# Expert rows gathered as quarters of a row and turned by VectorE, down weights copied by VectorE and ScalarE and asked for one expert later

## The reference, cut to what matters

```python
h_x = modulate(x, norm2_g[i], sf_x, cf_x).reshape(-1, d)      # rms_norm(x, g) * (1 + scale) + shift
scores = sigmoid(t @ router_w); _, idx = top_k(scores + router_bias, 8)   # 64 experts, 8 for each token
y = (silu(t[tok] @ w_gate[e]) * (t[tok] @ w_up[e])) @ w_down[e]           # expert width 256
routed = zeros((n_tok, d)).at[buf_tok].add(y * buf_w[:, None])
```

## Time and profile before

| | |
|---|---|
| median of 3 runs | 2725.13 us (2721.9 to 2731.74) |
| the profiled execution, own time | 2728.36 us |
| its span | 2726.7 us |
| phase `experts`, first ask for weights to last matmul | 1620.4 to 2590.6 |
| PE busy over the span | 91% |
| DMA | 410.21 MB, mean 150 GB/s over the span, some 340 GB/s in the expert phase |

### The profile page before, as it was taken

How to read it: one execution, slowest core, us unless ns; L and a number is a source line. 1 busy time by engine, 2 the same in 40 slices (tenths; PEclk the granted TensorE clock), 3 DMA queues, 4 the chain that set the end, 5 groups by cost and what they waited for, 6 DMA issues and landing times. The chain is left out here.

```text
span 2726.7 us, 72339 instructions
## 1 busy us (share of the span) xinstructions
PE 2492.2 (91%) x27195; PEld 1369.5 (50%) x27196; DVE 1518.7 (56%) x2653; ACT 975.3 (36%) x1707; POOL 842.9 (31%) x654
## 2 busy tenths in 40 slices
PE   5999899889799789899879779899999999999977
PEld 2448457735589645699834343333333333333333
DVE  3106355844477712676544476566666666666538
ACT  3613115512222113233211124455555555555411
POOL 1000000000155100111000005566666666666565
PEclk9999998989999999899979889999999999999989
DMA  6001402120000020000032328899988899684177
GB/s 251 15 0 48 143 16 93 49 64 16 1 4 4 3 75 1 2 5 5 6 137 93 128 103 317 333 352 357 358 337 328 331 343 346 252 312 142 70 282 295
DMA packets 109531, 410.21 MB, mean 150 GB/s; under 512 B 21049, under 2 KB 37131, under 8 KB 84236
## 3 DMA queue, kind: packets, MB, share of 16 engines
q1 hardware_dynamic: 77068, 289.81, 29.0%
q0 software_dynamic: 20736, 75.51, 7.4%
q10 hardware_dynamic: 11520, 41.95, 3.9%
HBM read 347.45 MB, written 59.77 MB: 149 GB/s over the span
## 5 line engine op out<-in xcount | busy, mean ns | idle before, releaser
L3282 PE MATMUL bank<-arena 128*32 x1280 | 568.9, 598 | 10.3 <-SPq L68 7.7
L3284 PE MATMUL bank<-arena 128*32 128x512 f32 x3840 | 570.0, 598 | 0.0
L3243 POOL COPY arena<-arena 128x2048 f32 x240 | 449.2, 1906 | 330.8 <-PE bank L3316 317.6
L3282 PEld LDWEIGHTS bank<-arena 128*32 128x32 f32 x1280 | 134.9, 110 | 359.3 <-issue 350.3
L3313 PE MATMUL bank<-arena 128*32 x640 | 289.3, 595 | 5.5 <-POOL arena L3243 5.5
L3316 PE MATMUL bank<-arena 128*32 128x512 f32 x1920 | 290.3, 595 | 0.0
L3437 DVE COPY arena<-arena 128x2048 f32 x80 | 138.7, 1734 | 203.4 <-PE bank L3284 189.3
L3374 ACT COPY arena<-arena 128x2048 f32 x80 | 152.2, 1902 | 168.5 <-PE bank L3284 141.9
L3233 POOL DMA_INDIRECT arena<-normed_rows,arena x80 | 165.0, 2063 | 118.6 <-DVE arena L3421 106.8
L1262 PE MATMUL bank<-arena 64*64 64x64 f32 x4480 | 165.4, 220 | 13.4 <-DVE arena L1334 5.4
L3313 PEld LDWEIGHTS bank<-arena 128*32 128x32 f32 x640 | 70.4, 110 | 197.8 <-issue 197.1
(11 more groups left out here) (553 smaller groups left out, 4625.7 us busy)
## 6 DMA issues: line engine op xcount, KB each, us to landing
arena<-in_exp_w_gate_dram SPq DMA_DIRECT2D x64, 1024.0 KB
arena<-in_exp_w_up_dram SPq DMA_DIRECT2D x64, 1024.0 KB
arena<-in_exp_w_down_dram SPq DMA_DIRECT2D x64, 1024.0 KB
expert_rows<-arena ACTq DMA_DIRECT2D x80, 512.0 KB
arena<-in_w_mod_dram SPq DMA_DIRECT2D x32, 512.0 KB, 7.7
arena<-in_x_dram SPq DMA_DIRECT2D x16, 512.0 KB
arena<-in_w_mod_dram SPq DMA_DIRECT2D x8, 1024.0 KB, 18.3
arena<-in_w_in_dram SPq DMA_DIRECT2D x12, 384.0 KB
```

Source lines behind the costliest of these rows:

```text
L3243: last = nc.gpsimd.tensor_copy(down_copy(u), down_of(slots[u]))
L3282: nc.tensor.matmul(out(SUB - 1), XTT[:, b.q, c, rows(SUB - 1)], W[:, :, c], start=first, stop=end)
L3284: last = nc.tensor.matmul(out(u), XTT[:, b.q, c, rows(u)], WC[:, u, :, c], start=first, stop=end)
```

## The change

- `mixed_out` puts scale and shift on each row before it is stored: two DVE operations of 128x1024 in place of one, with scale and shift spread over all partitions once at the start (16 matmuls, 8 copies by DVE, 8 by ACT). POOL then reorders each row into four quarters of 256 channels, grouped by `c` (128x1024, once per tile), and SP stores that. The copies out of PSUM lose their scale and shift.
- `IDX` holds four numbers for each row, one per quarter: 16 small DVE operations in place of one.
- In `experts`, POOL gathers 4 x 128 quarters of 1 KB per block, placed so that DVE's 32x32 transpose of 128x1024 gives the columns that `hidden` reads. PE's `turn` and both `flat_half` go.
- POOL's three copies of down weights go; DVE makes one (128x2048, at its step's end) and ACT two.
- SP asks for `down(e-1)` after the gates of `e` have landed, in place of `down(e)` before. At the start it asks for gates 0, down 0 and gates 1, and waits for the first gathered rows before the rest.

```diff
+    by_quarter = lambda row: row.rearrange("p (r i c) -> p r c i", r=SUB, c=KC)
+    packed = lambda row: row.rearrange("p (r c i) -> p r c i", r=SUB, c=KC)
...
+            for t in range(XT):
+                pool.wait_ge(xn, t + 1)
+                if t >= 2:
+                    pool.wait_ge(st[t % 2], 16 * (t // 2))
+                nc.gpsimd.tensor_copy(packed(XP[:, t % 2]), by_quarter(XN[:, t % 2])).then_inc(xp, 1)
...
                     if u >= 2:
                         dve.wait_ge(st[u % 2], 16 * (u // 2))
                         dve.wait_ge(xt, u - 1)
-                    nc.vector.tensor_scalar(XN[:, u % 2], X1[:, u], ri[:, u % 2], None, ALU.mult).then_inc(xn, 1)
+                    if u >= 2:
+                        dve.wait_ge(xp, u - 1)
+                    if u == 0:
+                        dve.wait_ge(mul_in, 1)
+                        dve.wait_ge(add_in, 1)
+                    chain(nc.vector.scalar_tensor_tensor(XN[:, u % 2], X1[:, u], ri[:, u % 2], MULS, ALU.mult, ALU.mult))
+                    nc.vector.tensor_tensor(XN[:, u % 2], XN[:, u % 2], ADDS, ALU.add).then_inc(xn, 1)
                     dve.wait_ge(xt, u + 1)
                     for c in range(KC // 2, KC):
...
+            quarters = IDX[:, 0:NBLK * SUB].rearrange("p (b q) -> p b q", q=SUB)
+            for q in range(SUB):
+                for r in range(SUB):
+                    last = TS(quarters[r * BR:(r + 1) * BR, :, q], ps[0][q * BR:(q + 1) * BR, 0:NBLK], float(SUB),
+                              float(r), ALU.mult, ALU.add)
+            chain(last)
...
     masks = Carve(cr.arena, P)
-    G, XTT, YB = cr.take(2, D), cr.take(2, KC, P), masks.take(2, D)
+    G, XTT, YB = cr.take(2, SUB, D // SUB), cr.take(2, D), masks.take(2, D)
     WC, WDC = cr.take(SUB - 1, 2, KC, ED), cr.take(SUB - 1, 2, D)
     HT, SG, H = masks.take(2, 2, P), masks.take(2, ED), masks.take(2, ED)
-    ID = cr.take(2, 1).bitcast(I32)
+    ID = cr.take(2, SUB).bitcast(I32)
+    row_quarters = xn_dram.rearrange("t (r n) -> (t r) n", r=SUB)
...
+    def columns(b, u, c):
+        at = ((u + 1) % SUB * KC + c) * BR
+        return XTT[:, b.q, at:at + BR]
...
     def slot_of(eng, b, u):
         n = eng.value_load(TAB[0:1, bass.ds(b.n * SUB + u if u else b.n * SUB, 1)], min_val=0, max_val=RING - 1)
         return bass.ds(n, 1)
@@ -3158,53 +3197,58 @@
             def at(i, n):
                 return i * ROUND + n if n else i * ROUND
 
-            def follow(j, i):
-                e, gates, downs = FROM + j, i * DRING, i * RING
+            def gates(i, e):
                 copied, read = released(at(i, e - RING))
                 hold(sp, hi_d, copied)
                 hold(sp, hi_a, copied)
                 hold(sp, up, read)
                 gate_up(bass.ds(at(i, e), 1), e % RING)
-                hold(sp, down_in[(e - 1) % DRING], downs * 16 + (16 * ((e - 1) // DRING) + 16))
+
+            def gates_landed(i, e):
+                hold(sp, loaded[e % RING], i * (DRING * 32) + 32 * (e // RING + 1))
+                sp.sem_inc(arrived, 1)
+
+            def downs(i, f):
+                if f >= DRING:
+                    copied, read = released(at(i, f - DRING))
+                    hold(sp, dcopy_d, copied)
+                    hold(sp, dcopy_a, copied)
+                    hold(sp, dn, read)
+                down(bass.ds(at(i, f), 1), f % DRING)
+
+            def down_landed(i, f):
+                hold(sp, down_in[f % DRING], i * (RING * 16) + 16 * (f // DRING + 1))
                 sp.sem_inc(down_arrived, 1)
-                copied, read = released(at(i, e - DRING))
-                hold(sp, dcopy, copied)
-                hold(sp, dn, read)
-                down(bass.ds(at(i, e), 1), e % DRING)
-                hold(sp, loaded[e % RING], gates * 32 + (32 * (e // RING) + 32))
-                sp.sem_inc(arrived, 1)
-
-            ROUND, FROM = RING * DRING, DRING
+
+            def follow(i, e):
+                gates(i, e)
+                down_landed(i, e - 2)
+                gates_landed(i, e)
+                downs(i, e - 1)
...
+            gate_up(bass.ds(0, 1), 0)
+            down(bass.ds(0, 1), 0)
+            gate_up(bass.ds(1, 1), 1)
+            sp.wait_ge(g_in[0], 16 * SUB)
+            downs(0, 1)
+            gate_up(bass.ds(2, 1), 2)
+            gates_landed(0, 0)
+            down_landed(0, 0)
+            gates_landed(0, 1)
+            gates_landed(0, 2)
+            for e in range(RING, FROM):
+                follow(0, e)
...
             def gather(b):
                 hold(pool, idx, b.n + 1)
-                nc.gpsimd.indirect_dma_start(
-                    out=G[:, b.q], out_offset=None, in_=xn_dram,
-                    in_offset=bass.IndirectOffsetOnAxis(ap=ID[:, b.q], axis=0)).then_inc(g_in[b.q], 16)
-
-            def copy_down(b, n=1):
-                slots = [down_slot_of(pool, b, u) for u in range(SUB - 1)]
-                hold(pool, down_arrived, count_of(pool, b, SUB - 2))
-                if n:
-                    hold(pool, dn, b.n + 1)
-                for u in range(SUB - 1):
-                    last = nc.gpsimd.tensor_copy(down_copy(u), down_of(slots[u]))
-                last.then_inc(dcopy, 1)
+                for q in range(SUB):
+                    nc.gpsimd.indirect_dma_start(
+                        out=G[:, b.q, q], out_offset=None, in_=row_quarters,
+                        in_offset=bass.IndirectOffsetOnAxis(ap=ID[:, b.q, q:q + 1], axis=0)).then_inc(g_in[b.q], 16)
 
             for n in range(4):
                 gather(Turn.at(n))
-            copy_down(Turn.at(0), 0)
-            gather(Turn.at(4))
-            with pool.Fori(0, TRIPS - 2) as t:
+            with pool.Fori(0, NBLK // 2 - 2) as t:
...
             def widen(b):
                 slot = down_slot_of(pe, b, SUB - 1)
                 hold(pe, down_arrived, count_of(pe, b, SUB - 1))
-                hold(pe, dcopy, b.n + 1)
+                hold(pe, dcopy_d, b.n + 1)
+                hold(pe, dcopy_a, b.n + 1)
                 hold(pe, hto, b.n + 1)
                 hold(pe, ya, b.n + 1)
...
+            def copy_downs(b, n=1):
+                slots = [down_slot_of(act, b, u) for u in (1, 2)]
+                hold(act, down_arrived, count_of(act, b, 2))
+                if n:
+                    hold(act, dn, b.n + 1)
+                nc.scalar.copy(down_copy(1), down_of(slots[0]))
+                nc.scalar.copy(down_copy(2), down_of(slots[1])).then_inc(dcopy_a, 1)
 
...
+            def turn(b, n=1):
+                hold(dve, g_in[b.q], b.half * 64 + 64)
+                if n:
+                    hold(dve, up, b.n)
+                nc.vector.transpose(XTT[:, b.q], G[:, b.q].rearrange("p q n -> p (q n)")).then_inc(turned, 1)
+
+            def copy_down(b, n=1):
+                slot = down_slot_of(dve, b, 0)
+                hold(dve, down_arrived, count_of(dve, b, 0))
+                if n:
+                    hold(dve, dn, b.n + 1)
+                nc.vector.tensor_copy(down_copy(0), down_of(slot)).then_inc(dcopy_d, 1)
 
             def index(b):
-                nc.vector.tensor_copy(ID[:, b.q], IDX[:, bass.ds(b.n, 1)]).then_inc(idx, 1)
...
-                    flat_half(b3)
+                    turn(b3)
                 if b5 is not None:
                     index(b5)
+                copy_down(b1)
...
```

More of the change, by code:

```diff
@@ L2736, in turn @@
                 last.then_inc(yt, 1)
+            for n, cols in enumerate((k.mul_col[1][0], k.add_col[1][0])):
+                for c in range(KC):
+                    last = nc.tensor.matmul(ps[4 + 2 * n + c // 4][:, (c % 4) * P:(c % 4 + 1) * P],
+                                            cols[:, c:c + 1].to_broadcast([P, P]), k.ident, start=True, stop=True)
+                last.then_inc(spread, 1)
             turn(0)
@@ L2773, in turned @@
                 nc.scalar.copy(YT[:, t % 2, 0:256], ps[0][:, 0:256]).then_inc(ya, 1)
+            act.wait_ge(spread, 2)
+            for c in range(KC):
+                last = nc.scalar.copy(ADDS[:, c::KC], ps[6 + c // 4][:, (c % 4) * P:(c % 4 + 1) * P])
+            last.then_inc(add_in, 1)
             turned(0)
@@ L2799, in turned @@
                 nc.vector.tensor_copy(YT[:, t % 2, 256:512], ps[1][:, 0:256]).then_inc(yd, 1)
+            dve.wait_ge(spread, 1)
+            for c in range(KC):
+                last = nc.vector.tensor_copy(MULS[:, c::KC], ps[4 + c // 4][:, (c % 4) * P:(c % 4 + 1) * P])
+            last.then_inc(mul_in, 1)
             turned(0)
@@ L3281, in chunk @@
                     first, end = c == 0, c == KC - 1
-                    nc.tensor.matmul(out(SUB - 1), XTT[:, b.q, c, rows(SUB - 1)], W[:, :, c], start=first, stop=end)
+                    nc.tensor.matmul(out(SUB - 1), columns(b, SUB - 1, c), W[:, :, c], start=first, stop=end)
                     for u in range(SUB - 1):
-                        last = nc.tensor.matmul(out(u), XTT[:, b.q, c, rows(u)], WC[:, u, :, c], start=first, stop=end)
```

(1 more changed line is left out.)

138 lines of the change are left out of this document (44 added, 94 removed).

## The result

| | before | change |
|---|---|---|
| median | 2725.9 us (5 runs) | 2841.5 us (2836.7 to 2846.4) |
| ratio | | 1.0409 [1.0388, 1.0430] |
| the same two kernels measured again (e1) | 2725.6 us | 2851.2 us, 1.0459 [1.0426, 1.0493] |
| span of the profile | 2726.7 us | 2842.4 us (e1) |

The change is slower, by 116 us. The profile taken with the first measurement fell into an execution of 12,010 us at a granted clock of 0.19 and says nothing, so the profile after is that of e1, the same kernel.

A forecast was written before the change was run, and what follows sets the result against it. The prediction took PE and the transfers to be balanced in the middle, and PE alone to bind past 2310 us. It summed 94 - 19 + 8 + 3 + 2.5 = +88.5 us on 2728.4, and forecast 2814 us, range 2695 to 2885.

The forecast's parts named there:

- The hole (+94): Small experts, 1684 to 2310 us: late asks leave q1 empty 5.0 us an expert, 14.1 us against 12.27, +94 us.
- The 12.8 us: Cycle per small expert if a transfer's whole fixed cost is about 2.0 us; the sum some 66 us lower.
- PE outside the middle (-19): From 2310 to 2590 us PE binds; 21 turns without transposes save 0.90 us each, -19 us.
- the zero for ACT: Expert turns: ACT's load with two more copies, 10.1 us, fits beside 10.87 and 14.1, so costs nothing.
- the rival without a hole: Middle stretch: transfers bind as now, the cycle stays about 12.0 to 12.3 us an expert, 2720 us; chance 0.15.
- Rival, PE still binds (2662): Middle stretch: the hole is covered, the cycle stays under 11.3 us an expert, 2662 us; chance 0.15.
- Quarters (+8): Expert gathers: 1 KB packets in place of 4 KB rows cost more DMA time, +8 us (0 to 17).
- mixed_out and table (+5.5): Ahead of the experts: added DVE and POOL work in the last tile +3 us, 16 small table operations +2.5 us.
- Start (0): Start of the expert phase: SP's wait for the first gather against 16 transposes no longer awaited, 0, +-5 us.
- POOL (9.9 or 11.0 us a turn): Expert turns: four gathers take POOL 9.9 us, or 11.0 if DVE's copies lengthen them; below the forecast cycle of 14.1.
- Low clock (2941): Middle stretch: every expert's wait drops PE to its low clock, some 2.5 us more a cycle, 2941 us; chance 0.05.

The follow-up runs named there:

- e3: The kernel before with one part alone, down(e-1) asked for only after the gates of e have landed: 2805.0 us, 1.0287.
- e2: The change with SP's asks, the first ones too, in the order of the kernel before: 2773.2 us, 1.0161.
- e5: The change with SP's asks as before, and ACT's table loads for its two copies of down weights put ahead of its store: 2706.6 us, 0.9924.
- e10: The change with SP's asks as before, and the table loads of ACT, PE and SP put ahead of their waits or work: 2682.7 us, 0.9842.
- e7: The change with SP's asks as before and one gather of whole 4 KB rows a block for four of quarters (channels misordered): 2765.0 us, 1.0130.
- e11: The change with its own late order of asks, and the table loads of ACT, PE and SP put ahead: 2737.3 us, 1.0028.

## Why the prediction was right, and where it was not

Forecast 2814 us in 2695 to 2885, slower at 0.70; measured 2841.5. Sign, mechanism and range held. Step by step, against the profile of e1:

- **The hole (+94): right.** 14.07 us an expert for a forecast of 14.1. The hole seen was 4.0 us at 150 GB/s and 1.0 more at 184, for 5.0 at 130. Its parts came out otherwise, and their errors nearly cancel: 3.1 us from last byte to ask for 1.0 + 1.7, and 1.65 from ask to full flow for 2.3. In the rows of before, the reading of the last byte took all of the flow up to 2003.0 for q1's; q1 had nearly run dry at 2002.0, and the rest were gathers (0.37 MB on q0 from 2002 to 2003). In us it gave 82.9 over 52 experts, quarters included, for 94 and 8, because the base was 12.48 and not 12.27 (the larger experts past 2310 us belong to it). e3 has it alone at 79 us, e1 less e2 at 78. The 12.8 us that the prediction drew from a fixed cost of 2.0 us took the shorter hole off and left out that less of q0 and q10 then fits into it: by its own working the estimate is (4.21 - 3.7 x 0.13)/0.391 + 3.7 = 13.2 us, and a sum 44 us lower, not 66. The fixed cost of about 2.0 us is what the Trainium skill (DMA: Bandwidth & Descriptors, Anatomy of one DMA) gives for transfers that GpSimd issues, and these are SP's. The trace does not agree for this chain: with SP's step at the 1.7 us of before, the rest of the hole is an estimated 3.1 - 1.7 + 1.65 = 3.05 us, and the cycle was 14.07.
- **PE outside the middle (-19): wrong, by 34 us, and with it the zero for ACT.** The tail grew by 15.4. The step that failed is "Both fit beside 10.87 and easily beside 14.1, so I cost them at nothing". ACT's 10.1 us was a sum of busy times (8.9 in the turn shown). The turn of ACT is a ring: its work, 1.15 us for DVE's half of the store, 0.6 for PE and 2.1 us of table loads and waits, 12.2 to 12.4 in all (the instructions overlap by some 0.4). The remark that ACT would be late next "with under 2 us to spare" named the engine, but counted no idle time that the engine makes itself. e5 shows it: the 2 us away, the turns are 10.87 to 10.97, as forecast. The middle hid the same fault: e2, without the late asks, would still have been at 12.83 us an expert and not at the 12.0 to 12.3 of the rival without a hole.
- **Rival, PE still binds (2662):** did not happen. e10 comes to 2682.7 with both obstacles gone, at 11.83 us an expert for 11.3.
- **Quarters (+8):** 8 us by e7, not clear of the noise.
- **mixed_out and table (+5.5):** +8.1 (of it the table, 4.91 us for 16 operations against 0.24 [4.7 for a forecast of 2.5, at 0.31 us each and not 0.11 to 0.24], and 3.45 ahead of it, the start of the table's writing against that of before, for 3). Over all profiles of either sort the mean is +11.4, so some 3 us more may be true.
- **Start (0): +9.4.** In e1 SP waited 9.0 us for the first gather before it asked for down 1 and gates 2. e2, which has neither that wait nor late asks, has 64.0, as before. The two were not separated; e3, with late asks from the 7th expert on and no such wait, has 65.9, and e11, with the wait and shorter steps, 66.6.
- **POOL (9.9 or 11.0 us a turn): too high.** A gather took 1277 ns on average, not 2182; the shortest took 942, the longest 2432. That it starts at another moment against DVE's copies, now that POOL's own are gone, was not separated. The Trainium skill (SBUF — State Buffer, SBUF: two separate sides) has a lock that a copy of DVE can hold against GpSimd, and the rows agree in kind: a gather of 1.82 us in e1 (2427.06) ran beside a copy of DVE (2427.53), two of 0.95 beside none. By these numbers it is an estimated 4 x (1.28 - 0.95) = 1.3 us of POOL a turn, and of the time no more than the 8 us of e7.
- **Low clock (2941):** no; the granted clock was 0.95 in the middle, against 0.99 before.

The terms that missed make the difference: 2.6 (ahead) + 9.4 (start) + 34.4 (tail) - 19.1 (middle) = 27.3 us, which is what the forecast of 88.5 lacks to 115.8. So the mechanism of the large term was right, but that the figure came within 28 us was in part luck: the middle came out 19 us under its forecast and the tail 34 us over, and inside the hole two misreadings nearly cancelled.

## What to carry to other kernels

An engine that works in order is late by its ring, not by its busy time: add to its work each wait in it and the time in which its queue reads tables or goes through waits with registers, which the timeline of the engine shows only as idle "on issue". Put such loads ahead of a wait that stands there anyway; here 2 us of them moved by two lines were worth 66 us. And a queue that waits for one transfer before it asks for the next needs something else in flight, enough for the whole step from last byte to next flow (here 4 to 5 us).

## What was not expected of the hardware

- In e2, three table loads and two waits with register values took ACT 2.12 us in one turn; over 80 turns the idle time on issue ahead of that copy was 155.1 us, 1.94 each:

```profile
L3366 ACT COPY arena<-arena x80: 1897/1900/1908, 1663.8 to 2639.0; 128x2048 f32 x80
its engine sat idle before it (us, times) until:
  issue: 155.1, 80
```

The engine's timeline has nothing in these 2 us. The view by the line of the table lookup does (L3166, two of the three):

```profile
L3166 ACTq FUSED_REGOPS  x312: 46/152/158, 1662.3 to 2638.1; - x156
L3166 ACTq TENSOR_LOAD <-arena x160: 272/278/1423, 1662.0 to 2637.2; - x160
```

A load took 278 ns as a rule, and the register operations behind it 152. The Trainium skill (Perfetto Trace Analysis, Sequencer-only Instruction) says of instructions of the sequencer that the profile holds their execution, not the wait ahead nor the semaphore's way after. The rows agree: the executions are there. Three loads at the usual 278 ns are 0.83 us of the 1.94; how the rest divides among register operations and waits was not measured.

- Ahead of `hidden`, PE stood idle on issue for 0.27 to 0.80 us in a turn of e2 and for 0.1 us in every second turn of e5, with the same table loads in its queue. That they cost nothing as long as matmuls are queued ahead of them is my reading.
- DVE's transpose of 128x1024 took 1.23 us, close to the 1.4 of two of 128x512.
